# Moving the output's copies and sums by one step in the attention units of a two-layer encoder

## The reference, cut to what matters

```python
# group A: 8 query heads on 2 key/value heads; B: 4 heads; C: 4 heads with two maps each
p = softmax_f32(logits, scale, v.dtype)                  # A and B
o = jnp.einsum('bkgqs,bskd->bqkgd', p, v)
...
p = jax.nn.softmax(logits + bias, axis=-1)               # C
a = (p[:, :, 0] - lam * p[:, :, 1]).astype(v.dtype)
return jnp.einsum('bhqs,bshe->bqhe', a, v)
...
x = x + jnp.concatenate([o_a, o_b, o_c], axis=-1) @ w_out[l]
```

## Time and profile before

| | |
|---|---|
| runs, median (range) | 3246.41 us (3244.54 to 3246.54) |
| profiled execution | 3244.24 us, of which the span is 3242.4 us |
| TensorE busy (matmul) | 3017.4 us, 93% of the span |
| DVE / ScalarE / GpSimd busy | 2086.2 / 1340.3 / 442.7 us |
| attention, first layer | about 290 to 790 us |
| attention, second layer | about 1870 to 2375 us |
| chain that ended last | PE 73%, issue 12%, DVE 7%, ACT 4%, POOL 3% |

### The profile page before, as it was taken

The page is one execution under the profiler, slowest core; times in us unless marked ns, Lnnn a source line. Parts: engine busy times, 40 slices in busy tenths (PEclk is TensorE's granted clock), DMA queues, the critical chain, the costliest instruction groups (busy, mean ns, idle before and its releaser), DMA issues.

```text
span 3242.4 us, 40207 instructions
## 1 busy us (share of the span) xinstructions
PE 3017.4 (93%) x13560; PEld 2320.5 (72%) x13560; DVE 2086.2 (64%) x2453; ACT 1340.3 (41%) x1837; POOL 442.7 (14%) x229
## 2 busy tenths in 40 slices
PE   6997988998999999999989888899989999999997
PEld 5685743676778888888867665357767788888886
DVE  5775788786255565555666668878842665656556
ACT  3224777786241222222323267778832322122214
POOL 3111122111410000000121112212124000000002
PEclk8998999999999999999989989999999999999998
DMA  5353322332121112111135433223221111111112
GB/s 174 133 162 104 89 58 50 75 82 85 40 65 40 52 39 65 39 52 39 39 114 178 149 82 73 62 58 78 59 98 46 52 52 52 52 39 50 53 39 65
DMA packets 269393, 237.80 MB, mean 73 GB/s; under 512 B 67648, under 2 KB 236352, under 8 KB 269248
## 3 DMA queue, kind: packets, MB, share of 16 engines
q1 hardware_dynamic: 269248, 235.99, 26.2%
HBM read 185.09 MB, written 50.86 MB: 73 GB/s over the span
## 4 chain that ended last, share of the span: by engine, by line
PE 73%; issue 12%; DVE 7%; ACT 4%; POOL 3%; DMA 1%; SPq 0%; ACTq 0%; DVEq 0%; POOLq 0%
PE ps L1579 27%; PE ps L1594 14%; PE ps L1348 12%; PE ps L1447 7%; PE ps L1494 4%; PE ps L1470 2%; ACT prob L833 2%; DVE ptl L1186 2%; PE ps L1475 1%; PE ps L1474 1%; PE ps L1564 1%; POOL prob L632 1%; ACT pth L865 1%; POOL rstd L589 1%; DVE ps L1137 1%
## 5 line engine op out<-in xcount | busy, mean ns | idle before, releaser
L1447 PE MATMUL ps<-stack 128*128 128x512 f32 (+1 forms) x1152 | 345.5, 421 | 76.2 <-ACT prob L833 61.5
L833 ACT ACTIVATE prob<-ps,nmx 128x1024 f32<-128x1024 f32 x320 | 356.6, 1114 | 69.5 <-DVE nmx L1141 32.2
L1266 DVE TENSOR_TENSOR xT<-ps,xT 128x512 f32<-128x512 f32 x352 | 241.1, 690 | 203.8 <-PE ps L1594 203.5
L1494 PEld LDWEIGHTS ps<-cst,prob 128*128 128x128 f32 x2048 | 238.8, 141 | 181.7 <-DVE ptl L1186 64.2
L1494 PE MATMUL ps<-cst,prob 128*128 128x128 f32 x2048 | 319.5, 279 | 33.0 <-DVE ptl L1186 27.2
L1186 DVE TENSOR_TENSOR ptl<-ps,pth 128x512 fp32r<-128x512 f32 x384 | 260.5, 687 | 117.9 <-ACT pth L865 113.9
L1447 PEld LDWEIGHTS ps<-stack 128*128 128x128 f32 (+1 forms) x1152 | 211.1, 195 | 172.0 <-ACT prob L833 115.4
L600 POOL TENSOR_TENSOR w0l<-wraw,w0h 128x1024 fp32r<-128x1024 f32 x34 | 84.5, 2489 | 1611.6 <-ACT w0h L712 1611.6
L1348 PE MATMUL ps<-xgh,w0h 128*128 128x512 f32 x768 | 252.7, 411 | 35.6 <-POOLq L231 10.1
L1231 DVE SCALAR_TENSOR_TENSOR cv<-u,vec,cv 128x1024 f32<-128x1024 f32 x176 | 225.9, 1283 | 90.8 <-ACT cv L938 80.4
L1579 PE MATMUL ps<-xgh,w0h 128*128 128x512 f32 x704 | 274.1, 389 | 2.4 <-ACT sq L930 2.4
(11 more groups left out here) (195 smaller groups left out, 5685.2 us busy)
## 6 DMA issues: line engine op xcount, KB each, us to landing
wraw<-in_w_up SPq DMA_DIRECT2D x88, 512.0 KB, 4.6
draw<-in_w_down SPq DMA_DIRECT2D x22, 1024.0 KB, 5.1
wraw<-in_w_in SPq DMA_DIRECT2D x36, 512.0 KB, 4.1
stack<-ka_d SPq DMA_DIRECT2D x64, 256.0 KB, 5.6
vst<-v_d SPq DMA_DIRECT2D x48, 256.0 KB, 3.8
x_d<-xT SPq DMA_DIRECT2D x2, 4096.0 KB, 18.3
qa_d<-rg SPq DMA_DIRECT2D x16, 512.0 KB, 2.7
wraw<-in_w_out SPq DMA_DIRECT2D x16, 512.0 KB, 5.4
```

The lines of the kernel that those rows point to most:

```text
L833: act.activation(two(dst), ps[:, 2 * (i % 2):2 * (i % 2) + 2, :], ACT.Exp, bias=nmx[:, b, i:i + 1], scale=scale, accum_out=rsum[:, b, i:i ...
L1266: ins = dve.tensor_tensor(xs, ps[:, 4 + j % 4, :], xs, ALU.add)
L1447: ins = pe.matmul(ps[:, 2 * (i % 2) + kh, :], st[q][0:rows, c0:c0 + P], st[k][0:rows, kh * HALF:(kh + 1) * HALF], start=n == 0, stop=n == ...
L1494: ins = pe.transpose(ps[:, 4 + s % 2, m * P:(m + 1) * P], prob[:, b, m, s * P:(s + 1) * P], ident)
```

## The change

Three numbers in `act_unit` and one in `dve_unit`: `copy_part` goes from step 2 to step 3, `hi_mix` and `copy_norm` from step 6 to step 7, `sum_output` from step 3 to step 4. No instruction is added, removed or changed, and TensorE's, GpSimd's and the DMA queues' streams are the same.

```diff
@@ act_unit, lines 865 to 875
                         for i in EXP_STEP_OF[nx["items"]].get(s, ()) if nx else ():
                             exp_item(nx, i)
-                        if s == 2 and prev:
+                        if s == 3 and prev:
                             copy_part(prev)
                         if s == 3 and nx and nx["group"] == "C":
                             scale_map(nx)
-                        if s == 6 and prev:
+                        if s == 7 and prev:
                             hi_mix(prev)
-                        if s == 6:
+                        if s == 7:
                             copy_norm(x)
@@ dve_unit, lines 1189 and 1190
-                        if s == 3 and prev:
+                        if s == 4 and prev:
                             sum_output(prev)
```

## The result

The changed kernel takes 3260.83 us (median of 5 runs, 3256.67 to 3262.70) against 3246.41 us (5 runs, 3242.22 to 3249.55): 1.0043 times as long, 95% interval 1.003 to 1.0056. The profiled execution of it took 3259.76 us, its span 3258.0 us.

What follows compares the result with a forecast made beforehand. TensorE, busy 93% of the span, was taken as the bound, only its gaps movable. B +4.8, A -1.4, C +5.8, units 7 and 8 +3.2 gave +12.4 us, median 3258, range 3248 to 3267.

Steps and rivals of the forecast that it cites:

- B: Units 1 to 6 of each layer: a DVE gap ahead of `ptl` 4 delays step 7; 12 x 0.4 = +4.8 us.
- C: Units 9 to 14: the sum between mixing 1 and maximum 6 delays DVE's chain; +5.8 us over both layers.
- A: Units 17 to 30: DVE's gap moves from `ptl` 3 to `ptl` 4; 28 x -0.05 = -1.4 us.
- units 7 and 8: Copy ahead of the map's scaling delays GpSimd's addition: unit 8 +1.3, unit 7 +0.3, both layers +3.2 us.
- Rival 1: No measurable change: a hidden wait absorbs B's delay, C at half; about +3 us, 3249; chance 0.20.
- rival 2: Faster: `ptl` 0, not exponential 0, sets item 2's start; -6 to -8 us, 3239; chance 0.08.
- the tail: `hi_mix` and `copy_norm` behind `pth` 7: A's 0.25 us wait at step 2 goes, valued at nothing behind exponential 0.
- unit 14: C's unit 14 of both layers: +0.5 us each, as TensorE's longer scores of A cover some.
- A gap of 0.35 is exchanged for one of about 0.3: A units: DVE's 0.35 us wait ahead of `ptl` 3 goes, about 0.3 opens ahead of `ptl` 4; -0.05 a unit.
- The bound of 0.12: A units: one register operation on ScalarE or DVE, 0.12 us either way; 28 x 0.12 = 3.4 us.

## Why the prediction was right, and where it was not

The time came out where the forecast had it, 3260.8 for 3258, for the reason given in B and C. But two terms are wrong, A by +7.3 us and units 7 and 8 by -3.4, and they cancel in part; that the total still came within 3 us is in part luck. Rival 1 fails in B, where each of the 12 units grew by 0.44 us; rival 2 in A, which became longer, and in the tail alone, which leaves A's unit at 12.89. The bounds of the terms add up to +5.5 and +20.5 (with 1.0 for unit 14), not to +5 and +18.

*B: right.* +0.44 us a unit for 0.4, by the forecast mechanism: a hole ahead of `ptl` 4 (0.49 for 0.35), then `ptl` 5 and step 7 late. The copy alone costs B nothing, as the sum stands in the hole; the sum alone costs 0.16, with a hole of 0.15; together they cost 0.44, with one of 0.49. The forecast kept the whole delay of step 7; it is 0.56 (from item 2's load to that of step 7: 353.46 - 346.14 = 7.32 us for 350.50 - 343.74 = 6.76), and 0.12 of it comes back before the next item 2. So 0.4 was right in part because the hole was put too small and the loss kept too whole.

*A: the wrong sign.* The step that failed is "A gap of 0.35 is exchanged for one of about 0.3", from which "I take -0.05 us a unit" follows. It is exchanged for 0.48. I had the copy 0.49 us behind `pth` 3, the spacing of two `pth` in a row; it came 0.62 behind (659.17 to 659.79), as the copy of line 849 does in every trace where it follows a `pth` without a longer wait. Two more links grew: maximum 3 follows the sum by 0.72 us (661.76 to 662.48), where it followed `ptl` 4 by 0.61, and `ptl` 5 follows maximum 3 by 1.25 us for 1.13 (655.73 to 656.86 before). The bound of 0.12 was called the cost of a register operation. That reading is wrong: by the listings of the change a register operation stands between two `pth` in a row, 0.49 apart, and none between the copy and `pth` 3, 0.61 apart. 28 x 0.21 = +5.9 us for -1.4, beyond the bound of 3.4. Such a sum is a difference of two times of half a microsecond, and a tenth in each link of the chain decided its sign. The bound should have been one such tenth for each link on the path, not one in all. The larger point is behind it: the copy's move was worth -0.36 us by itself, and the sum's move cost all of that and 0.21 more. I worked out only the two together and did not see that half of the change would be a gain.

*Tail: right.* 0, hidden by exponential 0, as said. The kernels with exponential 0 at step 0, with and without the tail, show that this was the cover: without it the tail is worth 20 us.

*C: right in its mechanism, with luck in the number.* +5.3 us for +5.8 up to unit 15; 20.46 us from addition to addition for the forecast 20.6. The sum pushes 0.60 us and not 0.69, and units that run at full clock before and after grow by 0.50 to 0.55 (9, 10 and 13 of the second layer). The clock moved others by more: unit 13 of the first layer grew by 2.2 us as it fell (0.99 to 0.88), unit 9 shrank by 0.7 as it rose (0.94 to 1.00). Two layers of C scatter by up to 3 us that way, so a match to 0.5 is in part chance. That mixing 3 could be held by GpSimd's `xgl` the forecast didn't consider; it had that collision for the mixing in unit 7 alone. It would have cost some 4 us had the tail not moved too.

*Units 7 and 8: wrong.* +3.2 forecast, -0.2 measured. The copy does delay the scaling of the map, but in unit 7 the held mixing, which GpSimd no longer holds, was worth more than that delay; the forecast had it worth less, at +0.3 us net. The kernel before at that place:

```profile
408.86 1.26 POOL L619 TENSOR_TENSOR osum<-osum,nrm 64x512 f32<-64x512 f32 x1 [0.22 <-POOL prob L632]
408.88 2.32 DVE L1155 SCALAR_TENSOR_TENSOR prob<-prob,rinv 128x1024 f32<-128x1024 f32 x1
```

After, that mixing takes 1.28 us. What the copy's place does there is better read from the whole change with C's sum at step 3: units 6 to 9 take 127.1 us over both layers, 2.3 less than before; moving C's sum adds 2.1 and gives the 129.2. The -0.2 itself is -1.27 in the first layer and +1.05 in the second, and the clock goes the same way: the mean granted in units 6 and 7 was 0.89 and 0.82 before and 0.93 and 0.92 after in the first layer, 1.00 and 0.93 before and 0.95 and 0.84 after in the second. How much of each number is the clock's the runs don't separate.

*Not in the sum at all:* +1.3 us between units 15 and 17. The kernel with C's sum alone doesn't have it (26.95 us a layer there, as before), the one with all but C's sum does (27.60): it comes with the changes in A and B, mostly with the sum (27.46 with the sum alone, 26.94 with the copy alone), all of it in unit 16, and I had counted from 17. At +0.64 us that unit pays three times what a later one does; why was not followed.

What stays open: one C unit a layer, 11, takes 21.1 us at full clock after the change, for 20.5 in units 9 and 10 and 20.8 in 12. Its mixing 2 comes 5.86 us behind mixing 1 where units 9 and 10 have 5.20; before it was 4.96 and 4.61. Part of it was there before: DVE stands for 0.45 us (0.46 after) ahead of maximum 7 with no releaser shown. The sum adds 0.84 us there (497.46 to 498.78 to 499.50, for 1.20 from mixing 1 to maximum 6 before) where it adds 0.60 elsewhere. No run was made for it.

## What to carry to other kernels

A change of several small moves is several changes. Here one line of it cost more than the whole, the other two were a gain, and a part that measures as nothing alone (the tail) was worth 20 us as soon as the wait in front of it was gone: test the parts in pairs, not only one at a time. When an operation is moved off one engine's path, ask which hole it leaves or fills on the engine that waits: the copy's delay was harmless only while the sum stood in it. Read a wait of TensorE in the row of the weight loads before calling a stretch full.

The best version that came of it, copy and tail moved, the sum left, exponential 0 a step earlier, takes 3197.93 us (3195.98 to 3198.66), 1.5% less than the kernel before.

## What the runs showed of the hardware

- A stretch in which the matmul row is 97% busy (83.87 of 86 us) could be shortened by 5%: from 13.94 to 13.24 us a unit. The matmul row showed 0.41 us of idle at the wait that went, the row of the loads 0.85, and the gain was 0.70.
- Who is held in a collision of DVE and GpSimd turned on hundredths of a microsecond: DVE's mixing took 2.32, 2.33 and 2.18 us for its 1.28 when GpSimd had begun 0.02, 0.03 and 0.19 us before it; GpSimd's operation took 2.33 and 1.96 us for 1.27 when DVE had begun 0.11 and 0.45 us before it. Of the 237 such pairs in the fourteen traces, one goes the other way: DVE was held (2.36 us) though it shows as 0.01 us ahead.
- On ScalarE two `pth` copies (128x512) start 0.49 us apart, and a `pth` and the 64x512 copy of line 849 0.61 to 0.62 on either side, though the smaller takes as long (0.59 us). It is not the shape or the change of line alone: the 64x512 copy of line 854 follows a `pth` by 0.48 to 0.50 in some units and by 0.61 to 0.63 in others, and a `pth` follows line 840 by 0.48. What makes the difference is not shown.
